# Streaming a table in transfers of two blocks instead of one, inside a decoder step on one core

## The chip, the cores and the metric

The kernel runs on one core of a Trainium2 chip. Its metric is the device time of one execution in microseconds (us). Three executions of the kernel before took 3694.8, 3695.88 and 3690.24 us, a median of 3694.8 us. A further execution was recorded by the hardware profiler; all rows shown here are of that one.

## The reference

One layer of a decoder is computed for 1024 prompt tokens and 64 sample tokens (8 sequences of 8) of width 1024. Two token mixers (a retention and a gated linear recurrence) are merged, projected and added to the input. Then comes the part that matters here, a retrieval from two tables of 16384 rows of 1024 float32 numbers, `peer_u` and `peer_v`. Each token selects 128 rows by the scores of its 8 heads, and the layer adds a weighted sum of the selected rows of `peer_v`:

```
s1, s2 = scores of the two halves of each head's query with 128 keys each
expert = 128 * e1 + e2          # the 16 best pairs of each of 8 heads: 128 rows per token
act = gelu(einsum('td,tkd->tk', x, u_tab[expert]))
out = einsum('tk,tkd->td', g * act, v_tab[expert])
x = x + g2 * out                # and a final normalisation by the row's mean square
```

## The kernel before

The kernel is a program written by hand for each engine, with semaphores between them: TensorE (PE), VectorE (DVE), ScalarE (ACT), GpSimd (POOL) and SyncE (SP), which issues most transfers. The mixers and the projections take the first part. The retrieval is spread over the whole second half.

**First table, rows by index.** POOL issues one indirect DMA for each token slot of a tile of 128 tokens (`gather`, L1472 to L1486): 128 rows of 4 KB, 512 KB in all, into one of 6 buffers `rows`. DVE multiplies each with the token's vector and sums (`dot`, L1689). There are 1088 of these for `peer_u`. For the sample tokens and the last two tiles of prompt tokens the second table is used in the same way: 320 more gathers, from `peer_v`, whose rows DVE adds up with their weights (`vrow`, L1699). The order of these jobs between DVE's other work is fixed by the table `stages()`.

**Second table, streamed.** For the other 768 prompt tokens, in 3 groups of 256 (`NDG` = 3, `GT` = 256), the whole table `peer_v` is read once in each group, as 128 blocks of 128 rows, and multiplied on PE with a matrix `W` that holds, for each row of the table, the weight that each of the 256 tokens gives it. One block is `vbuf[:, s, :]`, 128 partitions by 1024 numbers, 4 KB per partition. There are `VB` = 4 such buffers, used in turn. PE's `block_steps` (L2266) waits for the block's transfer on the semaphore `v_in[s]` (L2268), multiplies it in 8 pieces (L2273, `vacc<-W,vbuf`; the profile counts two matmuls for each), and then raises `v_used`. Over the 3 groups that makes 384 blocks, 96 turns of a loop over 4.

`W` is made as the stream runs. For each step of 4 tokens DVE and ACT build one-hot matrices (L1763, L1768, L2023, L2026), PE multiplies them in 12 small matmuls (`batch`, L2260, `scat`), and ACT copies the result into `W` (L2030). PE's order is: one block, one such batch, one block, and so on, in the first 320 blocks. The last 64 blocks (the second half of the last group) have no batch between them.

**SP's stream.** `v_stream` (L1373) holds the loop that issues the transfers. For buffer `s` it waits until the block that stood there has been used (L1376), and issues the next 512 KB (L1377). `v_used` starts at 4, so the first four are issued at once. Between parts of the stream SP issues other transfers on the same queue: a tile of `htok` (L1371), and in the last two groups the output of the group before (`y_store`, L1385, 1 MB) and the load of the next residual (`x3_load`, L1381, 1 MB), each 5 and 2 loop turns before a group's end; in the last group also two loads for the sample tokens (L1440, L1441) after 20 turns.

**The end.** After its last block PE multiplies the sample tokens' sums (L2390), for which DVE waits (L1832) before it goes on with its rows of `peer_v`; some 200 gathered rows are still to be added then, and two tiles to be finished.

Of the kernel before, what the change touches and what calls it, by code (L numbers as in the profile page):

```python
# [27 lines left out]
P = 128  # L28
D = 1024
# [16 lines left out]
NKEY = 128  # L46
# [24 lines left out]
VB, SB, VD = 4, 4, 6  # L71
QB = P // SB
# [157 lines left out]
def program(nc, I, O, S):  # L230
# [3 lines left out]
    def sem(name):  # L234
        return ctx.enter_context(nc.semaphore(name))

    def sb(c, name, shape, dt=F32):
        return c.enter_context(nc.sbuf_tensor(name, shape, dt))
# [17 lines left out]
    def hold(eng):  # L256

        eng.sem_inc(hold_sem, 1)

    with ctx:  # L260
# [43 lines left out]
        vbuf = sb(ctx, "vbuf", [P, VB, D])  # L304
# [964 lines left out]
        scaled2, q_ps, qh_ready, s_ps, s_ready, tr_ready, tr_free = (sem(n) for n in ("scaled2", "q_ps", "qh_ready", "s_ps", "s_ready", "tr_ready", "tr_free"))  # L1269
        tk, dk, pos_ready, hot_ready, idx_ready, max_ready, exp_ready = (sem(n) for n in ("tk", "dk", "pos_ready", "hot_ready", "idx_ready", "max_ready", "exp_ready"))  # L1270
        landed = [sem(f"landed{i}") for i in range(VD)]
        h_in, v_in = [sem("h_in0"), sem("h_in1")], [sem(f"v_in{i}") for i in range(VB)]
        used, v_used, gelu_ready, tr4_ready, picks_ready, oh_ready, sc_ps, w_evac, vacc_ready, ev_ready = (sem("s4_" + n) for n in (
            "used", "v_used", "gelu_ready", "tr4_ready", "picks_ready", "oh_ready", "sc_ps", "w_evac", "vacc_ready", "ev_ready"))
        x2g_in, sq4_ready, sums_ready, rs_ready, y_ready, y_out, ef_ready, acc_ready, oh2_ready, abs_ready, eq_ready = (sem("s4_" + n) for n in (
# [10 lines left out]
        def batch0(i):  # L1286
            return (i - FIRST_Q) * QB
# [64 lines left out]
        with nc.Block() as block:  # L1352
            @block.sync
            def _(sp):
# [17 lines left out]

                def v_stream(g, lo, hi):  # L1373
                    with sp.Fori(lo, hi) as i:
                        for s in range(VB):
                            sp.wait_ge(v_used, g * NKEY + i * VB + (s + 1))  # L1376
                            sp.dma_start(vbuf[:, s, :], I["peer_v"][bass.ds((i * VB + s) * P, P), :]).then_inc(v_in[s], 16)  # L1377

                def x3_load(g):
                    c0 = XG[g][0]  # L1380
# [52 lines left out]
                for g in range(NDG):  # L1433
                    h_load(2 * g + 3)
                    v_stream(g, 0, cut)
                    if g < NDG - 1:
                        h_load(2 * g + 4)
                    else:
                        sp.wait_ge(idx_ready, NUNIT)
                        sp.dma_start(spare, S["sums"]).then_inc(sum_out, 16)  # L1440
                        sp.dma_start(xs, S["x2"][:, :, FIRST:TA].rearrange("k p t -> p k t")).then_inc(xs_in, 16)  # L1441
                    if g:
                        v_stream(g, cut, end - 5)
                        y_store(g - 1)
                        v_stream(g, end - 5, end - 2)
                        sp.wait_ge(y_out, g * 16)
                        x3_load(g)
                        v_stream(g, end - 2, end)
                    else:
                        v_stream(g, cut, end)  # L1450
# [726 lines left out]
            def _(pe):  # L2177
# [75 lines left out]
                def batch(b, q, banks=scat):  # L2253
                    h = q % 2
                    pe.wait_ge(oh_ready, b + 1)
                    pe.wait_ge(oh2_ready, b + 2)
                    pe.wait_ge(w_evac, b + 1)
                    for n in range(SB):
                        for j in range(3):
                            mm = pe.matmul(banks[h][:, n * HK:(n + 1) * HK], oh2[:, h, n, :], oh1w[:, h, j, n // 2, :, n % 2], start=(j == 0), stop=(j == 2), skip_group_check=True)  # L2260
                    mm.then_inc(sc_ps, 1)

                def quarter(i4, scattering, inside=None):
                    g, q4 = divmod(i4, 4)

                    def block_steps(i, clear):  # L2266
                        for s in range(VB):
                            pe.wait_ge(v_in[s], g * (16 * NKEY // VB) + i * 16 + (q4 * (16 * QB // VB) + 16))  # L2268
                            e1 = slice(s, s + 1) if clear else bass.ds(i * VB + (q4 * QB + s), 1)
                            for k in range(KC):  # L2270
                                if clear and s == 0 and g and k % 2 == 0:
                                    pe.wait_ge(ev_ready, 4 * g + k // 2 - 3)
                                mm = pe.matmul(vacc[:, k, :], vbuf[:, s, k * P:(k + 1) * P], W[:, e1, :].rearrange("p o t -> p (o t)"),  # L2273
                                               start=(clear and s == 0 and k % 2 == 0), stop=False, skip_group_check=True)
                            mm.then_inc(v_used, 1)
                            if scattering:
                                batch(batch0(i4) + i * VB + s, s)
                    lo = 0
                    if q4 == 0:
                        block_steps(0, True)  # L2280
                        lo = 1
                    if inside is not None:
                        hold(pe)
                        with pe.Fori(lo, TURN_AT // VB) as i:
                            block_steps(i, False)
                        lo = TURN_AT // VB
                        inside()
                    hold(pe)
                    with pe.Fori(lo, QB // VB) as i:
                        block_steps(i, False)  # L2290
# [165 lines left out]
```

## Time and profile before

| | |
|---|---|
| median of 3 executions | 3694.8 us (3690.24 to 3695.88) |
| profiled execution, its own time | 3689.39 us |
| its span, first to last instruction | 3687.6 us |
| PE, DVE, POOL, ACT busy | 85%, 79%, 53%, 36% of the span |
| moved by DMA | 1127.21 MB, 305 GB/s read from and written to HBM over the span |
| of it the stream of `peer_v` | 384 transfers of 512 KB |
| mean granted clock of TensorE | 0.93 of full speed |

How to read it: the stream begins at 1752.6 us, PE's first block at 1770 us, and its last block ends at 3374 us. What bounds the kernel differs between the stretches inside this time, so each is read alone. Idle time of an engine matters only where what it waits for, or who waits for it, sets the end.

### The profile page before, as it was taken

Reading aid. Unit: us, or ns where it says so; the run is one execution under the profiler, and the core shown is the slowest. Engines: PE = TensorE matmul, PEld = TensorE weight load, DVE = VectorE, ACT = ScalarE, POOL = GpSimd, SP = SyncE. Lnnn points to the kernel's source line nnn. Section 1 sums busy time; section 2 is a strip of 40 time slices with the busy share of each in tenths; the row PEclk is TensorE's granted clock in tenths of the full one; section 3 lists DMA queues with packets and bytes.
Section 4 is the critical chain, followed back from the end, with each engine's and each line's share of the span. In section 5 each row is a group of like instructions: output and inputs, shape, how many; then the busy total and the mean of one; then the engine's idle time right before and its main releaser. Section 6 shows DMA issues by size and latency. Waiting matters only on the chain.

```text
span 3687.6 us, 56423 instructions
## 1 busy us (share of the span) xinstructions
PE 3124.7 (85%) x17498; PEld 2479.9 (67%) x17498; DVE 2906.8 (79%) x6210; ACT 1341.4 (36%) x2988; POOL 1954.9 (53%) x1504
## 2 busy tenths in 40 slices
PE   7999999999999989588899999999988999995000
PEld 4777776666666658477778788778877888884000
DVE  3333347998888877888899999999999887667898
ACT  4333311222222221178555555555555565000000
POOL 0000013454466654454677776767766766676676
PEclk9999999999999999799999999999999999997555
DMA  7444454777788898777999999999999999999998
GB/s 258 140 135 130 137 161 140 243 230 239 237 293 291 293 322 299 278 265 265 356 396 385 387 372 398 367 363 389 384 346 379 371 408 405 402 411 350 344 352 305
DMA packets 435382, 1127.21 MB, mean 306 GB/s; under 512 B 41888, under 2 KB 174368, under 8 KB 435232
## 3 DMA queue, kind: packets, MB, share of 16 engines
q0 software_dynamic: 204800, 745.10, 54.7%
q1 hardware_dynamic: 225664, 370.51, 28.2%
q10 hardware_dynamic: 4768, 9.96, 0.7%
q8 instruction: 49, 0.80, 0.1%
q14 instruction: 101, 0.83, 0.1%
HBM read 1098.81 MB, written 26.62 MB: 305 GB/s over the span
## 4 chain that ended last, share of the span: by engine, by line
PE 36%; DVE 24%; issue 13%; DMA 9%; POOL 3%; ACT 1%; DVEq 0%; ACTq 0%; POOLq 0%; SPq 0%
PE vacc L2273 16%; DVE rows L1689 10%; PE vacc L863 8%; DMA rows<-in_peer_u,eidx 5%; PE scat L2207 3%; DVE oh1w L1768 2%; PE vacc L834 2%; POOL rows L1486 2%; PE vacc L2187 2%; DMA rows<-in_peer_v,eidx 1%; DMA vbuf<-in_peer_v 1%; DVE eidf L1581 1%; PE scat L2260 1%; DVE htok L1699 1%; DVE hot L1675 1%
## 5 line engine op out<-in xcount | busy, mean ns | idle before, releaser
L1486 POOL DMA_INDIRECT rows<-in_peer_u,eidx x1088 | 1424.7, 1309 | 959.8 <-DVE dots L1689 602.6
L2273 PE MATMUL vacc<-W,vbuf 128*128 (+1 forms) x6144 | 1422.6, 387 | 34.3 <-DMA vbuf<-in_peer_v 23.2
L1689 DVE CUSTOM_DVE_ANT_0 rows<-rows,htok 128x1024 f32<-128x1024 f32 x1088 | 1349.9, 1269 | 126.3 <-DMA rows<-in_peer_u,eidx 115.4
L2273 PEld LDWEIGHTS vacc<-W,vbuf 128*128 128x128 f32 x6144 | 1154.9, 192 | 184.3 <-issue 36.1
L2023 ACT ACTIVATE oh<-iota,e2s 128x128 bf16<-128x128 f32 x1536 | 486.4, 391 | 17.0 <-DVE wpart L1739 9.8
L863 PE MATMUL vacc<-W 128*128 128x384 f32 x1280 | 435.1, 496 | 1.2 <-ACTq L763 1.2
L1470 POOL TENSOR_TENSOR hot<-hot,cid 128x864 f32<-128x864 f32 x68 | 129.2, 1903 | 543.3 <-DVE hot L1675 542.0
L1699 DVE SCALAR_TENSOR_TENSOR htok<-rows,dots,htok 128x1024 f32<-128x1024 f32 x256 | 328.8, 1284 | 72.9 <-DMA rows<-in_peer_v,eidx 66.3
L1486 POOL DMA_INDIRECT rows<-in_peer_v,eidx x256 | 310.4, 1212 | 121.4 <-issue 88.1
L863 PEld LDWEIGHTS vacc<-W 128*128 128x128 f32 x1280 | 242.8, 193 | 168.3 <-issue 9.5
L2030 ACT ACTIVATE W<-scat 128x256 f32 (+1 forms) x320 | 122.6, 383 | 580.7 <-PE scat L2260 534.1
L2026 ACT ACTIVATE oh<-oh,ones 128x512 bf16<-128x512 bf16 x384 | 277.2, 722 | 12.5
L1768 DVE TENSOR_TENSOR oh1w<-oh,wpart 128x768 bf16<-128x768 bf16 x384 | 237.7, 619 | 45.4 <-PE scat L2260 25.7
L2207 PE MATMUL scat<-W 128*128 128x256 f32 (+1 forms) x1024 | 252.5, 403 | 5.4 <-DVE W L1566 5.4
L2260 PEld LDWEIGHTS scat<-oh1w,oh 128*128 128x128 bf16 x3840 | 154.5, 97 | 118.3 <-issue 72.1
L2207 PEld LDWEIGHTS scat<-W 128*128 128x128 f32 x1024 | 196.9, 196 | 44.9 <-issue 6.3
L2260 PE MATMUL scat<-oh1w,oh 128*128 128x64 bf16 x3840 | 167.5, 192 | 58.6 <-DVE oh1w L1768 49.0
L863 PE MATMUL vacc<-rows,W 128*128 128x320 f32 x640 | 179.8, 436 | 2.5 <-ACTq L763 2.5
L2299 PE MATMUL vacc<-ident,htok 128*128 128x128 f32 x16 | 3.9, 424 | 209.8 <-DVEq L1802 209.8
L834 PE MATMUL vacc<-W 128*128 128x256 f32 x768 | 169.4, 381 | 0.0
L252 ACT ACTIVATE W<-vacc 128x768 f32<-128x768 f32 x32 | 25.9, 811 | 379.4 <-PE vacc L863 365.1
L834 PEld LDWEIGHTS vacc<-W 128*128 128x128 f32 x768 | 146.7, 191 | 23.2 <-ACTq L801 1.6
(330 smaller groups left out, 3086.9 us busy)
## 6 DMA issues: line engine op xcount, KB each, us to landing
vbuf<-in_peer_v SPq DMA_DIRECT2D x384, 512.0 KB
W<-in_w_in SPq DMA_DIRECT2D x80, 512.0 KB, 7.5
W<-in_wq SPq DMA_DIRECT2D x64, 512.0 KB
vbuf<-in_w_ada SPq DMA_DIRECT2D x9, 2048.0 KB, 24.1
rows<-in_peer_u,eidx POOLq DMA_INDIRECT x1088
W<-in_w_in SPq DMA_DIRECT2D x16, 1024.0 KB, 6.7
W<-in_w_ada SPq DMA_DIRECT2D x3, 2048.0 KB, 19.2
W<-in_w_out SPq DMA_DIRECT2D x12, 512.0 KB
```

Of the source, the lines that this page charges most:

```text
L834: mm = pe.matmul(dst, z.hnT[:, k, t * P:(t + 1) * P], w_qkv[:, k, :], start=(k == 0), stop=(k == KC - 1))
L863: mm = pe.matmul(pslice(z, pj if bank == "pj" else pk, s), w_part[j - 1][:, k, :], z.hnT[:, k, lo:hi], start=(k == 0), stop=(k == KC - 1))
L1470: g.tensor_tensor(hot[:, t, :, :], hot[:, t, :, :], bc(cid[:, t, :], 1, [P, TOPK, NCAND]), ALU.mult).then_inc(hot_ready, 1)
L1486: g.indirect_dma_start(rows[:, s, :], None, table[:, :], bass.IndirectOffsetOnAxis(ap=picked, axis=0)).then_inc(landed[s], 16)
L1689: v.tensor_tensor_reduce(rows[:, s, :], rows[:, s, :], htok[:, home, :], 1.0, 0.0, ALU.mult, ALU.add, dots_of(t)[:, c:c + 1]).then_inc(use ...
L1699: v.scalar_tensor_tensor(acc[t], rows[:, s, :], w[:, c:c + 1], acc[t], ALU.mult, ALU.add).then_inc(used, 1)
L1768: v.tensor_tensor(oh1w[:, h, :, :, :, :], bc(oh1[:, j % EB, :, :, :], 1, shp), bc(wpart[:, u * QB + j, :, :, :], 3, shp), ALU.mult).then_i ...
L2023: ins = act.activation(oh2[:, h, n, :], iota[:, :], ACT.Abs, bias=e2s[:, bass.ds(k, 1)], scale=-1.0)
L2026: act.activation(oh2[:, h, :, :], oh2[:, h, :, :], ACT.Relu, bias=ones[:, 0:1], scale=-1.0).then_inc(oh2_ready, 1)
L2207: mm = pe.matmul(scat[u][:, 0:n], wq[j % 4][:, k, :], hn2T[g][:, k, 0:n], start=(k == 0), stop=(k == KC - 1))
L2260: mm = pe.matmul(banks[h][:, n * HK:(n + 1) * HK], oh2[:, h, n, :], oh1w[:, h, j, n // 2, :, n % 2], start=(j == 0), stop=(j == 2), skip_g ...
L2273: mm = pe.matmul(vacc[:, k, :], vbuf[:, s, k * P:(k + 1) * P], W[:, e1, :].rearrange("p o t -> p (o t)"), start=(clear and s == 0 and k % ...
```

## The change

The host lays out a second copy of the table's contents, `v_pairs`, in place of reading `peer_v` for the stream. In it the rows of two successive blocks that go to the same partition lie behind each other, so that one partition's part of a pair is 8 KB in one piece. SP issues one transfer of 1 MB for a pair of buffers where it issued two of 512 KB. A pair is issued when both of its buffers have been used. There are 2 semaphores `v_in` in place of 4, one for each pair, and PE waits on the one of the block's pair. The number of buffers, the order of the blocks and everything on the other engines stay.

```diff
-        h_in, v_in = [sem("h_in0"), sem("h_in1")], [sem(f"v_in{i}") for i in range(VB)]
+        h_in, v_in = [sem("h_in0"), sem("h_in1")], [sem(f"v_in{i}") for i in range(VB // 2)]
 ...
                 def v_stream(g, lo, hi):
                     with sp.Fori(lo, hi) as i:
-                        for s in range(VB):
-                            sp.wait_ge(v_used, g * NKEY + i * VB + (s + 1))
-                            sp.dma_start(vbuf[:, s, :], I["peer_v"][bass.ds((i * VB + s) * P, P), :]).then_inc(v_in[s], 16)
+                        for h in range(VB // 2):
+                            sp.wait_ge(v_used, g * NKEY + i * VB + (2 * h + 2))
+                            src = I["v_pairs"][bass.ds(i * (VB // 2) + h, 1)].rearrange("o p n -> p (o n)")
+                            sp.dma_start(vbuf[:, 2 * h:2 * h + 2, :].rearrange("p s n -> p (s n)"), src).then_inc(v_in[h], 16)
 ...
                         for s in range(VB):
-                            pe.wait_ge(v_in[s], g * (16 * NKEY // VB) + i * 16 + (q4 * (16 * QB // VB) + 16))
+                            pe.wait_ge(v_in[s // 2], g * (16 * NKEY // VB) + i * 16 + (q4 * (16 * QB // VB) + 16))
 ...
         "peer_u": a["peer_u"][0], "peer_v": a["peer_v"][0],
+        "v_pairs": a["peer_v"][0].reshape(NKEY // 2, 2, P, D).transpose(0, 2, 1, 3).reshape(NKEY // 2, P, 2 * D),
```

SP's instructions for one part of the stream (a load of `htok`, then the loop of one turn) stood before as follows; `ISA` is the wait with the address, `DMA` the issue.

```order
156 L1371 DMA htok<-scratch_hn 128x1024
157 L1374 UNCONDITIONAL_BRANCH
158 L1374 ISA
159 L1377 ISA
160 L1377 DMA vbuf<-in_peer_v 128x1024
161 L1376 REGISTER_ALU
162 L1377 ISA
163 L1377 DMA vbuf<-in_peer_v 128x1024
164 L1376 REGISTER_ALU
165 L1377 ISA
166 L1377 DMA vbuf<-in_peer_v 128x1024
167 L1376 REGISTER_ALU
```

The same place of the changed kernel, on SP:

```order
150 L1371 DMA htok<-scratch_hn 128x1024
151 L1374 UNCONDITIONAL_BRANCH
152 L1374 ISA
153 L1378 ISA
154 L1378 DMA vbuf<-in_v_pairs 128x2048
155 L1376 REGISTER_ALU
156 L1378 ISA
157 L1378 DMA vbuf<-in_v_pairs 128x2048
158 L1374 REGISTER_ALU
159 L1374 COMPARE_AND_BRANCH
```

Two issues stand in one turn of the loop where there were four; what stands ahead of and behind the loop is the same. On PE (the two first blocks of a turn, inside the loop) the instructions of before are these:

```order
711 L2273 ISA [waits v_in0]
712 L2273 MATMUL vacc<-W,vbuf 128x256 x8
717 L2273 ISA [waits v_in1]
718 L2273 MATMUL vacc<-W,vbuf 128x256 x8
```

and now:

```order
711 L2274 ISA [waits v_in0]
712 L2274 MATMUL vacc<-W,vbuf 128x256 x8
717 L2274 ISA [waits v_in0]
718 L2274 MATMUL vacc<-W,vbuf 128x256 x8
```

The matmuls stay in place; the second block of a pair waits on the same semaphore as the first.

## Rows read from the trace of the kernel before

**Rows 1.** Page, slices: busy tenths of the DMA engines in 40 slices of 92 us.

```profile
DMA  7444454777788898777999999999999999999998
```

**Rows 2.** Busy time by stretch: start:end, length, engines (instructions), clock, DMA share, GB/s.

```profile
1760.00:2869.00 1109.00, 1031.24 (x7255) 883.02 (x7255) 1049.38 (x2496) 604.37 (x1579) 769.72 (x571) 0.99 0.98 377
2869.00:3125.00 256.00, 255.03 (x1808) 221.07 (x1807) 203.12 (x353) 147.87 (x381) 173.24 (x134) 0.99 1.00 395
3125.00:3375.00 250.00, 229.29 (x1034) 199.96 (x1033) 158.32 (x195) 2.21 (x4) 173.91 (x123) 0.96 1.02 403
3375.00:3688.00 313.00, 20.68 (x89) 17.41 (x88) 272.60 (x252) 8.07 (x12) 213.69 (x189) 0.52 0.90 328
```

**Rows 3.** Waits of PE alone from 2869 to 3374 us: total us, times, longest.

```profile
PE vacc L2273 <- DMA vbuf<-in_peer_v: 20.7, 3, 7.9
...
```

**Rows 4.** Chain that ended last, around PE's late blocks: start, length, what.

```profile
3170.17 15.38 DMA vbuf<-in_peer_v
...
3275.21 17.50 DMA vbuf<-in_peer_v
...
3326.45 17.90 DMA vbuf<-in_peer_v
...
3374.24 1.75 PE tps L2390 x16
```

**Rows 5.** The same chain by line, from 1760 to 2868 us (first lines' start).

```profile
by line: DVE rows L1689 21.2%; issue 19.7%; DMA rows<-in_peer_u,eidx 17.8%; PE vacc L2273 14.2%; DVE oh1w L1768 6.3%; POOL rows L1486 2.6%; DVE hot L1675 2.3%; DVE oh L1763 2.2%; DVE eidf L1581 2.0%; PE scat L2260 1.7%; DVE ti L1634 0.9%; D
```

**Rows 6.** DVE in order of time, the row after PE's last block.

```profile
3376.01 0.69 DVE L1832 TENSOR_TENSOR hot<-tps,g2T 128x512 f32<-128x512 f32 x1 [8.51 <-PE tps L2390]
```

**Rows 7.** Issues of L1377 from 3005 to 3110 us, then 3190 to 3270 us.

```profile
L1377 SPq DMA_DIRECT2D vbuf<-in_peer_v x27: 332/333/333, 3006.3 to 3107.5; - x27
...
L1377 SPq DMA_DIRECT2D vbuf<-in_peer_v x23: 332/333/333, 3192.3 to 3268.3; - x23
```

**Rows 8.** PE's three waits for the stream, one window each (3165, 3270, 3325 us).

```profile
PE vacc L2273 <- DMA vbuf<-in_peer_v: 5.4, 1, 5.4
...
PE vacc L2273 <- DMA vbuf<-in_peer_v: 7.5, 1, 7.5
...
PE vacc L2273 <- DMA vbuf<-in_peer_v: 7.9, 1, 7.9
```

**Rows 9.** DMA issues: count, KB each, median us from issue to landing.

```profile
W<-in_w_in SPq DMA_DIRECT2D x16, 1024.0 KB, 6.7
W<-in_dmask SPq DMA_DIRECT2D x1, 512.0 KB, 4.8
```

**Rows 10.** DMA queues: packets, MB, share of 16 engines; 60 to 300, 2940 to 3125 us.

```profile
q1 hardware_dynamic: 42442, 30.99, 43.5%
...
q0 software_dynamic: 13889, 50.58, 68.9%
q1 hardware_dynamic: 6765, 24.64, 33.5%
```

**Rows 11.** Page, all packets of the run by size.

```profile
DMA packets 435382, 1127.21 MB, mean 306 GB/s; under 512 B 41888, under 2 KB 174368, under 8 KB 435232
q8 instruction: 49, 0.80, 0.1%
q14 instruction: 101, 0.83, 0.1%
```

**Rows 12.** SP in order of time around an output store in the stream.

```profile
3272.30 0.40 SPq L1385 DMA_DIRECT2D out_y<-x  x1
3275.21 48.13 SPq L1377 DMA_DIRECT2D vbuf<-in_peer_v  x12
```

**Rows 13.** Waits from 1760 to 2869 us, of DVE and of PE.

```profile
DVE rows L1689 <- DMA rows<-in_peer_u,eidx: 43.1, 64, 5.7
...
PE scat L2260 <- DVE oh1w L1768: 48.5, 43, 6.5
PE vacc L2273 <- DMA vbuf<-in_peer_v: 2.5, 1, 2.5
```

## The prediction

> **What bounds the kernel now.** I read the slices first: from slice 20 on the DMA engines are 9 tenths or more busy [rows 1], so the stream of the table and the gathers share a full resource. By stretch [rows 2], the reader is to see three regimes. From 1760 to 2869 us DVE is busy 1049 of 1109 us and PE 1031. From 2869 to 3125 us PE is busy 255.0 of 256 us. From 3125 to 3375 us PE is busy 229 of 250 us, and DMA's share is 1.02. After that it is the tail of gathers.
>
> Then PE's waits: from 2869 us to its last block it waits for hardly anything but the stream, 20.7 us in 3 places [rows 3]. Then the chain: in the last stretch it runs through PE's blocks and these three transfers, up to L2390 at 3374.24 us [rows 4]. There DVE has stood idle for 8.51 us until PE delivers [rows 6], and what follows it is gathers and DVE work that the change does not touch. So from 2869 to 3374 us every microsecond that PE loses moves the end. Before 2869 us the chain is mixed, DVE's rows 21.2%, gathers' landings 17.8%, PE's blocks 14.2% [rows 5], and PE has slack.
>
> **PE's pace.** 27 issues of the stream from 3006.3 to 3107.5 us are 26 intervals of 3.89 us: one block with its batch. 23 issues from 3192.3 to 3268.3 us are 22 intervals of 3.455 us: one block alone [rows 7].
>
> **What the change takes from the stream: its lead.** A block's transfer is issued when the block four earlier is used, so it has three blocks' time until PE needs it. The three waits show the lead without batches exactly: transfers landing 15.38, 17.50 and 17.90 us after issue [rows 4] made PE wait 5.4, 7.5 and 7.9 us [rows 8], so the lead is 10.0 us, 0.35 under 3 x 3.455. Now a pair goes out when both its blocks are used, and its first block is needed two blocks later: 10.0 - 3.455 = 6.55 us without batches. With batches it is 2 x 3.89 = 7.8 us (the batch covers the 0.35).
>
> **What it adds: a longer transfer.** How long 512 KB of the stream take is in no row; in 13 of the last 16 turns of the loop PE did not wait, so under 10.0 us. I build it up. A packet's time: 42442 packets of 30.99 MB take 43.5% of 16 x 240 us, 39.4 ns at 730 bytes; 13889 packets of 50.58 MB take 68.9% of 16 x 185 us, 146.8 ns at 3642 bytes [rows 10]. The line through both is 12.4 ns + 0.0369 ns per byte: 164 ns for 4 KB, 315 ns for 8 KB. One engine of 16 moves 8 rows of a block. A transfer of 1 MB with no gathers beside it landed after 6.7 us [rows 9]; its data alone need 16 x 0.164 = 2.6 us, which leaves 4.1 us fixed. (The one of 512 KB after 4.8 us leaves 3.5.) Beside full gathers I let the two queues take packets in turn: a block needs 8 x (0.164 + 0.164) = 2.6 us, 6.7 in all; a pair in packets of 8 KB needs 8 x (0.315 + 0.164) = 3.8, 7.9 in all; a pair in packets of 4 KB 5.2, 9.3 in all. That nothing above 4 KB goes out on this kernel's data queues is seen in the page: just 150 packets have 8 KB or more, as many as the instruction queues have [rows 11]. So no row shows an 8 KB packet of data. I take 7.9, since the row is contiguous on both sides, and keep 6.7 and 9.3 as ends.
>
> The turn by packets is also what the Trainium skill states ("DMA: Bandwidth & Descriptors", section Queues, rings and completion order): each engine goes round its queues packet by packet. The rows agree in so far as both queues together make 102.4% of the engines' time [rows 10]; they don't show the order. The same page (Anatomy of one DMA) fits 2.0 us plus bytes at 436 GB/s, so a pair would land after 4.4 us and never be late. The trace's 1 MB took 6.7 us without contention [rows 9], so I go by the trace.
>
> **The sum.**
> (a) Last 64 blocks, 16 turns, 13 of them without a foreign transfer. A turn is two pairs. The first waits 7.9 - 6.55 = 1.35 us; the second has gained those 1.35 us of lead and waits for nothing; then the first is late again. 13 x 1.35 = +17.6 us. Ends: 13 x 0.15 = 2 and 13 x 2.75 = 36.
> (b) The 3 turns behind foreign transfers. SP issues the store at 3272.30 us and the block 2.9 us after it [rows 12]. The pair goes out 3.455 us later than that block did, but what it stands behind in the queue is the store, and PE needs its first block at the same moment; it lands later by its own extra 1.2 us only. 3 x 1.2 = +3.7. Ends 0 and 3 x 2.6 = 8.
> (c) 16 turns from 2869 to 3125 us: 7.9 - 7.8 = 0.1 each, +1.6. Ends 0 and 16 x 1.5 = 24.
> (d) Before 2869 us, 64 turns. At 0.1 us they are nothing beside PE's own idle time of 78 us [rows 2]. Two foreign transfers there cost PE 2.5 us before [rows 13], and get 1.2 us longer each; DVE, in front by up to a batch, takes most of it: +1. Behind PE's waiting block stand its next batch and so DVE's L1768, which waits for it; that is the price if the cover is gone. Upper end by 9.3 us: 64 x 1.5 = 96 us on PE, of which the chain's share of PE, 14.2 + 1.7% [rows 5], makes 15.
> (e) DMA time saved: 192 x 8 packets fewer on each engine, 1536 x 12.4 ns = 19 us over 1604 us, 13 of them before 2869 us. It helps where a landing binds, 17.8% of the chain [rows 5]: -2.3, rounded -3 with the halved number of issues. Lower end -13, since DVE waits 43.1 us for rows there [rows 13]. After 2869 us it helps nobody, since PE is the bound.
> SP's halved issues, at 0.33 us each [rows 7], cost nothing before or now: SP waits for PE between them.
>
> Sum: 17.6 + 3.7 + 1.6 + 1 - 3 = +21. On the profiled execution's 3689.4 us that is 3710; it lay 5.4 us under the median, and a median stands against a median, so the time is 3694.8 + 21 = **3716 us**.
>
> **Rivals.**
> *Packets of 4 KB.* If the 8 KB row is cut in two, a pair lands after 9.3 us: 36 + 8 + 24 + 15 + 1 - 3 = +81, 3776 us. For it: no data packet above 4 KB in the run [rows 11]. Against it: none was asked for. The Trainium skill ("DMA: Bandwidth & Descriptors", section SWDGE vs HWDGE vs iDMA) has a packet at preferably 4096 bytes at most, told of the software path; no run here shows it for SP's queue.
> *Gathers pushed aside.* An 8 KB packet of the stream holds a waiting gather packet up by 0.151 us more, 8 times, 1.2 us per pair. If DVE can't make it good in the second half of the pair, 138 pairs before 2869 us at the 17.8% of the chain that landings hold add 29 us: 3745. Against it: DMA's total is no larger, and six buffers smooth it.
> *No change.* If the fixed part under load is the 3.5 us of the smaller transfer [rows 9], a pair lands after 7.3: (a) is 13 x 0.75 = 10, (c) is 0, (b) and (d) 5, and (e) takes -10: +5, 3700.
> *Faster.* DMA is the true bound, at 0.98 to 1.02 in all three stretches [rows 2], and PE's busy time only follows it. Then the 19 us saved count nearly in full, once a pair lands under 6.55 us: +4 from (b), -17, that is -13: 3682 us. The point from which it decides is 6.55 us. Against it: PE's 255 of 256 us busy, and 6.7 us for 1 MB alone. The skill's rule to batch to 1 MiB and more (same page, Rules for kernel authors) speaks for it; this stream has no idle queue that larger transfers could fill.
>
> **Chances.** Forecast 0.55 (its own range 3704 to 3732), 4 KB packets 0.17, gathers pushed aside 0.09, no change 0.11, faster 0.08. The range that holds 8 in 10 reaches over the no-change case below and to the 4 KB case above: 3695 to 3780. A difference of 0.2%, 7.4 us, is about what can be told from none. Faster by more: 0.09; within: 0.15; slower by more: 0.76.
>
> **What would show it.** In the last stretch PE waits for `vbuf` about 16 times and not 3, near 1.35 us each, every second pair, and the three long ones grow by about 1.2. PE's last block ends near 3395 us, DVE's idle time at L1832 grows from 8.5 to about 30, and what comes after keeps its length. From 2869 to 3125 us PE stays near 3.89 us per block. Queue 1 shows packets of 8 KB with 315 ns; if they are of 4 KB, the 4 KB rival holds. If PE waits for nothing new and DVE's waits for rows fall, the forecast is wrong and DMA was the bound; if DVE's waits for rows rise before 2869 us, the gathers were pushed aside.

## The result, and the profile after

The changed kernel takes 3747.55 us (4 runs, 3746.25 to 3748.23) against 3694.81 before: a ratio of 1.0145, interval 1.013 to 1.0159, or 53 us more. The forecast was 3716 us, slower by 21, with a range of 3695 to 3780. The direction and the range held. The size did not: it was two and a half times the forecast. The profiled execution has a span of 3746.2 us, 58.6 more than the one of before.

The page of the changed kernel first: packets of all queues by size, the two data queues, and the stream's issues. The last two lines are the data queues of the kernel before.

```profile
DMA packets 407733, 1127.19 MB, mean 301 GB/s; under 512 B 38816, under 2 KB 171296, under 8 KB 383008
q0 software_dynamic: 204800, 745.10, 54.3%
q1 hardware_dynamic: 198016, 370.50, 27.5%
vbuf<-in_v_pairs SPq DMA_DIRECT2D x192, 1024.0 KB
...
q0 software_dynamic: 204800, 745.10, 54.7%
q1 hardware_dynamic: 225664, 370.51, 28.2%
```

Now 24725 packets have 8 KB or more, where there were 150 [rows 11]: 24576, which is 192 x 128, more than the instruction queues' 149. Each partition's 8 KB goes out as one packet, as forecast. Queue 1 (the stream's) fell from 28.2% of 3687.6 us to 27.5% of 3746.2 us, 10 us less for each of the 16 engines. Queue 0 (the gathers') went from 54.7% to 54.3%, which is 17 us more. (The shares are rounded, so each difference is good to about 4 us.) So the saving in packets is real, and it did not shorten the queues' work as a whole.

Busy time by stretch of the changed kernel, with the columns of [rows 2]. The stretches are PE's blocks 0 to 255 (two groups), 256 to 319 (third group, with batches), 320 to 383 (without), and the tail:

```profile
1772.00:2889.00 1117.00, 1034.92 (x7196) 884.93 (x7196) 1037.29 (x2464) 593.35 (x1550) 752.31 (x567) 0.98 0.96 371
2889.00:3159.00 270.00, 257.64 (x1807) 222.03 (x1808) 202.81 (x356) 151.84 (x392) 152.37 (x133) 0.99 0.98 379
3159.00:3433.00 274.00, 237.12 (x1029) 199.56 (x1028) 158.34 (x195) 2.52 (x4) 138.66 (x123) 0.95 0.93 369
3433.00:3746.00 313.00, 22.00 (x97) 18.36 (x95) 272.67 (x252) 8.07 (x12) 214.44 (x189) 0.53 0.91 328
```

The tail has kept its 313 us. The third group's second half took 274 us against about 250, its first half 270 against 256, and the two groups ahead of them 1117 against about 1098 (from 1770 to 2868 us before). PE is no longer busy all the time in the third group's first half, and DMA's share fell in every stretch ahead of the tail, by 0.02, 0.02 and 0.09.

PE's waits for the stream in the last stretch (total, times, longest), the three long ones and two turns of the loop, PE in order of time:

```profile
PE vacc L2274 <- DMA vbuf<-in_v_pairs: 36.6, 20, 8.4
...
3225.64 2.92 PE L2274 MATMUL vacc<-W,vbuf 128*128 x6 [5.33 <-DMA vbuf<-in_v_pairs]
...
3345.85 3.78 PE L2274 MATMUL vacc<-W,vbuf 128*128 x8 [7.67 <-DMA vbuf<-in_v_pairs]
...
3402.09 8.27 PE L2274 MATMUL vacc<-W,vbuf 128*128 x23 [8.40 <-DMA vbuf<-in_v_pairs]
```

```profile
3261.13 7.17 PE L2274 MATMUL vacc<-W,vbuf 128*128 x32 [0.93 <-DMA vbuf<-in_v_pairs]
3268.51 7.17 PE L2274 MATMUL vacc<-W,vbuf 128*128 x32 [0.21 <-issue]
3276.76 7.17 PE L2274 MATMUL vacc<-W,vbuf 128*128 x32 [1.08 <-DMA vbuf<-in_v_pairs]
3284.30 7.17 PE L2274 MATMUL vacc<-W,vbuf 128*128 x32 [0.37 <-DMA vbuf<-in_v_pairs]
```

The three long waits stayed what they were [rows 8], 5.4, 7.5 and 7.9 us then. The new waiting is in the other 17, 15.2 us. Each row of x32 is a pair: PE halts before each, about 1 us before one of a turn and 0.2 to 0.4 us before the other, and a turn takes 3276.76 - 3261.13 = 15.6 us where four blocks took 13.8.

The chain of the changed kernel in these stretches, start, length and what (a landing stands here only when PE waited for it):

```profile
3049.59 9.25 DMA vbuf<-in_v_pairs
3066.87 8.31 DMA vbuf<-in_v_pairs
...
3275.86 8.31 DMA vbuf<-in_v_pairs
3284.30 7.18 PE vacc L2274 x32
3291.65 8.01 DMA vbuf<-in_v_pairs
3299.80 7.18 PE vacc L2274 x32
3307.14 7.79 DMA vbuf<-in_v_pairs
```

The landings that PE waited for took 7.8 to 9.3 us in these rows, and 7.7 to 9.4 us in all of the third group, leaving out those behind a foreign transfer. How long the others took is in no row. And the place where DVE meets PE's last block, which answers to [rows 6]; ahead of it stand DVE's waits up to 2869 us (those of [rows 13] are 43.1 us, 64 times):

```profile
DVE rows L1690 <- DMA rows<-in_peer_u,eidx: 65.5, 60, 4.8
...
3434.79 0.69 DVE L1833 TENSOR_TENSOR hot<-tps,g2T 128x512 f32<-128x512 f32 x1 [43.88 <-PE tps L2391]
```

The last row and the one of before divide the loss. L1833 starts 58.8 us later than it did. 35.4 of them are DVE's longer idle time (43.9 against 8.5). The other 23.4 are DVE's own arrival: it came to this point at 3390.9 us and not at 3367.5, and its waits for gathered rows had grown by 22.4 us. So two paths became late, PE's more than DVE's. If PE's waits alone were taken away, DVE's 23.4 less the old slack of 8.5 should still move the end by 15 us; a run below tests this. The forecast had nothing there.

### The profile page after: what moved, and what is told of

Same layout as the page of the kernel before. It is cut to its first block, busy times and chain, and to the rows that moved or that the text cites. A ratio compares the mean times of both kernels' runs of the same rounds, so it can differ in the third digit from the quotient of the medians.

```text
span 3746.2 us, 55655 instructions
## 1 busy us (share of the span) xinstructions
PE 3147.2 (84%) x17498; PEld 2488.7 (66%) x17498; DVE 2905.0 (78%) x6210; ACT 1340.8 (36%) x2988; POOL 1898.4 (51%) x1504
## 3 DMA queue, kind: packets, MB, share of 16 engines
q0 software_dynamic: 204800, 745.10, 54.3%
q1 hardware_dynamic: 198016, 370.50, 27.5%
## 4 chain that ended last, share of the span: by engine, by line
PE 28%; DVE 21%; issue 17%; DMA 16%; POOL 3%; ACT 1%; SPq 0%; ACTq 0%; DVEq 0%; POOLq 0%
PE vacc L2274 10%; DMA rows<-in_peer_u,eidx 8%; DVE rows L1690 7%; PE vacc L863 7%; DMA vbuf<-in_v_pairs 5%; POOL rows L1487 3%; PE scat L2208 3%; PE vacc L834 2%; DVE oh1w L1769 2%; PE vacc L2188 2%; DMA rows<-in_peer_v,eidx 2%; DVE eidf L1582 1%; DVE htok L1700 1%; DVE oh L1764 1%; DVE hot L1676 1%
## 5 line engine op out<-in xcount | busy, mean ns | idle before, releaser
L1487 POOL DMA_INDIRECT rows<-in_peer_u,eidx x1088 | 1386.5, 1274 | 1026.2 <-DVE dots L1690 674.3
L2274 PE MATMUL vacc<-W,vbuf 128*128 (+1 forms) x6144 | 1440.0, 389 | 79.5 <-DMA vbuf<-in_v_pairs 65.4
L1487 POOL DMA_INDIRECT rows<-in_peer_v,eidx x256 | 292.4, 1142 | 170.0 <-issue 123.8
```

Of the source, the lines that this page charges most:

```text
L1487: g.indirect_dma_start(rows[:, s, :], None, table[:, :], bass.IndirectOffsetOnAxis(ap=picked, axis=0)).then_inc(landed[s], 16)
```

## The experiments

Theory A: a pair is issued too late and lands too late for PE. Rival B: the stream in pairs makes the gathers land late, and DVE with them. Each ratio is to the kernel before on the same chip.

**One half of the change, the late issue.**

```diff
-                            sp.wait_ge(v_used, g * NKEY + i * VB + (s + 1))
+                            sp.wait_ge(v_used, g * NKEY + i * VB + (2 * (s // 2) + 2))
```

> The kernel before with one edit: two transfers of 512 KB as before, but both are issued only when both buffers of the pair have been used. So the lead of a pair's first block falls by one block as in the change, the packets stay at 4 KB and PE still waits for each block alone. Theory A (the lead is too short for the landing, once per turn of the loop): the first block lands after about 6.7 us, against a lead of 6.4 us without batches and 7.6 with: 13 x 0.3 = 4 us in the last 64 blocks, little before, in all +3 to +10 us, 3698 to 3705. Rival B (packets of 8 KB hold up the gathers, the lead does not matter): 0, 3695. Rival C (the late issue by itself, whatever the size, is the loss): near the changed kernel, 3740 to 3750.

Measured: 3711.55 us, ratio 1.0053 (1.0035 to 1.0071), some 19 us. The late issue alone, at 4 KB and 512 KB, makes a good third of the change's loss. It is more than A's +3 to +10, B's zero is out, and so is C, the whole loss. PE's waits for the stream from 2880 us on:

```profile
PE vacc L2273 <- DMA vbuf<-in_peer_v: 29.4, 11, 9.8
```

**The other dose of lateness.** Each block one block later, nothing bunched:

```diff
-                            sp.wait_ge(v_used, g * NKEY + i * VB + (s + 1))
+                            sp.wait_ge(v_used, g * NKEY + i * VB + (s + 2))
```

> The kernel before with one edit: each block's transfer of 512 KB is issued one block later, so its lead is two blocks in place of three; nothing is bunched, packets stay at 4 KB. Theory A (lead against landing): a block lands after 6.7 us against 6.4 without batches, so PE waits 0.3 us once in three blocks of the last 64, 6 us, and the landings that lie above the median add as much again: +5 to +20 us, 3698 to 3713. If issuing two transfers at once was what cost the run with late issue its 19 us: 0 to +5.

Measured: 3712.88 us, 1.0057 (1.004 to 1.0074). The same loss with nothing bunched. PE waited 33.4 us in 13 places from 2880 us on, and DVE's waits for gathered rows stayed at 46.3 us up to 2900 us (before: 47.4). So a lead of two blocks does not suffice where PE sets the pace, even with a transfer of 512 KB. But it is only just too short for the stream's own blocks: 3.9 us in ten places here, and 2.9 us in eight in the run before this one. The three waits behind foreign transfers make the rest, 29.5 and 26.5 us where they were 20.7. (Here a foreign transfer is issued one block later as well.) DVE's arrival at L1832 was 3375.0 us with the late issue and 3367.7 here, against 3367.5 before. That does not yet show a cost of bunching, since DVE's arrival differs by up to 8 us between traces whose first two groups have the same stream.

**The packet size.** The changed kernel, reading the pair straight from the table:

```diff
-                            src = I["v_pairs"][bass.ds(i * (VB // 2) + h, 1)].rearrange("o p n -> p (o n)")
+                            src = I["peer_v"][bass.ds((i * VB + 2 * h) * P, 2 * P), :].rearrange("(s p) n -> p s n", p=P)
```

(the destination is `vbuf[:, 2 * h:2 * h + 2, :]` with its two rows apart).

> The changed kernel with one edit: a pair is read straight from the table as it was, two pieces of 4 KB per partition in one transfer of 1 MB, so packets should be of 4 KB. Lead as in the change. Theory A: a pair lands after 9.3 us and not 7.9, so PE waits 9.3 + 0.15 - 6.55 = 2.9 us in each of 13 turns of the last 64 blocks (38), about 1.7 in each of the 16 turns before (27), and some 0.9 of it shows in the 64 turns ahead (60): +125 us, 3820, range 3780 to 3850. Rival B (8 KB packets hold up the gathers): the gathers get half of each engine again, so it is faster than the changed kernel, 3700 to 3740.

Measured: 3770.97 us, 1.0221 (1.0197 to 1.0246), +78 us. The direction is A's: smaller packets, later landing, slower. The size is two thirds of what A said and lies below its range. That one wait per turn at full size counts too much once both pairs are late, since every wait lengthens the next lead, is my reading and not tested. By the ratios the layout by pairs is worth some 28 us against the same transfer without it (1.0221 against 1.0145), yet the pair costs more.

**Where it is lost.** Pairs in some groups only:

```diff
+        PAIRED = (0, 1)     # and (2,) in the second kernel
...
+                        if g in PAIRED:
+                            for h in range(VB // 2):
+                                sp.wait_ge(v_used, g * NKEY + i * VB + (2 * h + 2))
+                                src = I["v_pairs"][bass.ds(i * (VB // 2) + h, 1)].rearrange("o p n -> p (o n)")
+                                sp.dma_start(vbuf[:, 2 * h:2 * h + 2, :].rearrange("p s n -> p (s n)"), src).then_inc(v_in[2 * h], 16)
+                        for s in range(VB if g not in PAIRED else 0):
```

> Pairs in the first two groups of the stream only (256 blocks), single blocks in the third. Theory A in the size that the changed trace shows: PE is 21 us late at block 256 there, and nothing is added after it: +21 us, 3716 (3708 to 3722). If DVE sets the pace there and has slack for PE's waits: 0 to +5. If lateness made there is what makes the third group slow: +45 to +53.

> Pairs in the third group only (128 blocks), single blocks in the first two. Theory A: 13 us over the 64 blocks with batches and about 22 over the 64 without, +35 us, 3730 (3722 to 3738); with the run of pairs in groups 1 and 2 it adds up to the change's +53. My prediction's own terms (a), (b), (c) would give +23, 3718. Rival B: the gathers' delay counts where DVE is the bound, in the first two groups, so here only 0 to +10.

Measured: first two groups 3709.1 us, 1.0047 (1.0029 to 1.0065), +17; third group 3725.32 us, 1.0089 (1.0069 to 1.0108), +33. They add up to 50 of the change's 53, and each came out near what A said; for the first two groups that was for another reason, as the runs with constant tiles show. The third group's part is in PE's waits (42.0 us, 34 times, from 2880 us on) and in DVE's idle time for L2391's counterpart (39.5 us). In the first two groups PE waited too, 33.5 us in 34 places up to 2900 us, but what DVE waited for was rows (this profiled execution took 3717.04 us, 8 more than the median):

```profile
DVE rows L1695 <- DMA rows<-in_peer_u,eidx: 71.9, 64, 4.8
DVE oh1w L1774 <- PE scat L2266: 3.7, 4, 1.2
```

**PE's lead taken out of the question.** The long matmuls read a constant tile, so that the sum over the second table is left out; every transfer is made as before, and PE asks for the landing only ahead of the last matmul:

```diff
-                            pe.wait_ge(v_in[s // 2], ...)
...
+                                if k == KC - 1 and s % 2:
+                                    pe.wait_ge(v_in[s // 2], ...)
-                                mm = pe.matmul(vacc[:, k, :], vbuf[:, s, k * P:(k + 1) * P], ...
+                                mm = pe.matmul(vacc[:, k, :], ident[:, :], ...
```

> The changed kernel, with PE's long matmuls reading a constant tile in place of the streamed blocks (so the sum over the second table is left out), the transfers unchanged and issued as before; PE asks for a pair's landing only ahead of the last matmul of the pair's second block, 6.9 to 7.8 us later than it did. All DMA traffic, packets of 8 KB and late issue stay; only PE's short lead is taken away. To be compared with the same edit of the kernel before, which runs beside it. Theory A (PE's lead): the two are equal within 5 us, both near 3680 to 3690, since part of the three long waits goes too. Rival B (8 KB packets or bunched transfers hold up the gathers): this one stays 20 to 50 us above the other.

> The kernel before with the same edit (PE reads a constant tile, the sum over the second table is left out), the landing of each block asked for ahead of the block's last matmul. Three long waits of 5.4, 7.5 and 7.9 us become about 2, 4 and 4.5: 10 us less than before, 3685. Same under both theories; it is the level for the other run.

Measured: pairs 3703.24 us, 1.0025 (1.0013 to 1.0038); single blocks 3688.48 us, 0.9988 (0.9977 to 0.9998). So 15 us of the 53 stay when PE hardly waits for the stream (in the pairs' run 7.5 us in 3 places from 2880 us on), and 38 go. Both theories hold a part. The 15 us are the size worked out above from DVE's arrival, and the trace of the pairs' run agrees: DVE comes to L1833 at 3388.98 us without waiting for PE, where it came at 3390.9 in the changed kernel.

```profile
3388.98 0.68 DVE L1833 TENSOR_TENSOR hot<-tps,g2T 128x512 f32<-128x512 f32 x1
```

(The profiled execution of the single blocks was the slowest of its ten, 3701.55 us, so its trace is not set beside this one.) The same form for three more ways to move the table:

> The transfer of 1 MB in packets of 4 KB (pair read straight from the table), with PE's long matmuls reading a constant tile (the sum over the second table is left out) and PE asking for the landing only at a pair's end. It tells what the 15 us are that the changed kernel keeps in this form. Theory B8 (an 8 KB packet holds gather packets up): with 4 KB packets it falls to the level of single blocks in this form, 3688. Theory BB (1 MB at once, in whatever packets, bunches the gathers): it stays at 3703.

> Two transfers of 512 KB issued together when both buffers of a pair are used, in packets of 4 KB, PE's long matmuls reading a constant tile (the sum over the second table is left out), landing asked for ahead of each block's last matmul. Theory B8: 3688, since no packet is above 4 KB. Theory BB: 3700 to 3705, since the same 1 MB is queued at once; it should then equal the run with one transfer of 1 MB in 4 KB packets.

> Pairs in the first two groups only, PE's long matmuls reading a constant tile (the sum over the second table is left out), landing asked for ahead of the last matmul of a pair's first block. If the first two groups' 17 us come from gathers that land later while DVE sets the pace: 12 to 17 us over the single blocks in this form (3688), 3700 to 3706. If they come from PE's waits for the stream: 3688, +-4.

Measured: one transfer of 1 MB in 4 KB packets 3697.11 us, 1.0018 (1.0009 to 1.0028); two of 512 KB issued together 3694.73 us, 1.0015 (1.0003 to 1.0027); 8 KB pairs in the first two groups only 3705.12 us, 1.0045 (1.0028 to 1.0062). The last is as slow as the same pairs with PE reading them (1.0047), though PE waited for the stream 5.5 us up to 2900 us there and not 33.5. So the loss of the first two groups is not PE's waiting; it sits there and on the gathers' side. The two forms in 4 KB packets lie clear above single blocks (0.9988), by 11 and 10 us, and the intervals do not part them from the 8 KB form (1.0025, 14 us by the ratios). So most of what stays in this form needs no packet of 8 KB. One thing stays open: pairs in two groups only came out above pairs in all three. PE asks for the landing one block earlier there, and the intervals overlap.

**The first two groups alone, three forms on one chip.** The 8 KB kernel is the one above again; the others have the pair from the table in one transfer, and two transfers issued together:

```diff
-                            sp.wait_ge(v_used, g * NKEY + i * VB + (s + 1))
+                            sp.wait_ge(v_used, g * NKEY + i * VB + ((s + 1) if g == 2 else (2 * (s // 2) + 2)))
```

> Pairs in the first two groups only, each one transfer of 1 MB read straight from the table, in packets of 4 KB; single blocks in the third group. If 8 KB packets hold the gathers up: 0 to +6 us, though a pair lands about 1.3 us later and PE waits more often than with 8 KB. If 1 MB queued at once does it: +12 to +20. If PE's waits do it after all: above the run with 8 KB packets.

> Pairs of the changed kernel, in packets of 8 KB, in the first two groups only; the same kernel as in the earlier run of pairs in groups 1 and 2, here beside the two others on one chip. +17 us (+12 to +22).

> Two transfers of 512 KB issued together once a pair's two buffers are used, in the first two groups only; packets of 4 KB. If 8 KB packets are the cause: 0 to +4 us. If 1 MB queued at once is: +12 to +20, like the run with one transfer in 4 KB packets.

Measured: 1 MB in 4 KB packets 3725.73 us, 1.0095 (1.0082 to 1.0108); in 8 KB packets 3711.2 us, 1.0053 (1.0039 to 1.0066); two of 512 KB 3699.6 us, 1.0021 (1.0012 to 1.0029), which is +8 and lies between the two sizes expected. The first surprised me: in 4 KB packets the same transfer is worse here too. The chains of the 4 KB and the 8 KB form up to 2868 us, shares by line, say why:

```profile
by line: PE vacc L2281 45.5%; DMA vbuf<-in_peer_v 35.1%; issue 7.6%; PE scat L2266 3.2%; DVE rows L1695 2.1%; another core or an unknown queue 1.0%; DVE oh1w L1774 0.7%; SPq L1380 0.6%; DVE oh L1769 0.4%; DVE x L1802 0.3%; ACT L2020 0.2%; A
```

```profile
by line: DMA rows<-in_peer_u,eidx 30.3%; issue 28.7%; DVE rows L1695 12.3%; POOL rows L1492 6.5%; DVE oh1w L1774 3.4%; PE vacc L2281 2.7%; DVE eidf L1587 2.6%; DVE oh L1769 2.3%; DMA vbuf<-in_v_pairs 2.3%; DVE hot L1681 1.7%; DVE tv L1638 0
```

With 4 KB packets the bound passes to PE and the stream (81% of the chain), and PE waited for it 76.7 us in 52 places up to 2900 us. Before, DVE and its gathers held the larger part of a mixed chain [rows 5]. With 8 KB packets the stream is 2.3% of it and the gathers' landings are 30.3%, against 17.8 [rows 5]. DVE's waits for rows tell the same, of the 4 KB form first, then the 8 KB form, then two transfers together, up to 2900 us (before: 47.4 us, 69 times):

```profile
DVE rows L1695 <- DMA rows<-in_peer_u,eidx: 39.8, 44, 5.4
```

```profile
DVE rows L1695 <- DMA rows<-in_peer_u,eidx: 67.4, 59, 4.6
```

```profile
DVE rows L1689 <- DMA rows<-in_peer_u,eidx: 56.3, 65, 4.7
```

(In three other runs whose stream is that of before in these groups they were 50.5 to 53.9 us.) So 8 of the 20 us on this chip come with the late, bunched issue alone. The other 12 come with one transfer of 8 KB packets. They run through the gathers by the chain. That it is the packet's length that holds them up is not shown: the control with 4 KB packets is bound by something else here, and where PE reads a constant tile the packet size made no difference clear of noise.

**The three long waits, another place.** The foreign transfers (L1385, L1381, L1440, L1441) are issued from ACT:

```diff
-                        v_stream(g, cut, end - 5)
-                        y_store(g - 1)
-                        v_stream(g, end - 5, end - 2)
-                        sp.wait_ge(y_out, g * 16)
-                        x3_load(g)
-                        v_stream(g, end - 2, end)
+                        v_stream(g, cut, end)
```

> The kernel before, with the transfers that stand between the stream's on SP's queue (two loads for the sample tokens, the output stores of 1 MB and the loads of the next residual) issued from ACT, on its own queue. The stream is then not behind them in a queue. If the three waits of 5.4, 7.5 and 7.9 us come from standing behind in one queue: they go, 20.7 us of PE's chain, and with them 1 to 2 us each of low clock after them: 3665 to 3676. If they come from sharing the engines: nothing, 3695. ACT's queue as a third one in turn may also slow gathers: up to 3705.

> The changed kernel with the same move to ACT's queue. Theory A: the long waits go, the short one in every turn of the loop stays, so it gains about as much as the kernel before does by this edit, 20 to 27 us: 3722 to 3730, and stays some 50 us above the other run. If the loss of the change lay in the turns behind the foreign transfers, it would fall to the other run's time.

Measured: on the kernel before 3689.9 us, 0.9991 (0.9981 to 1.0001); on the changed kernel 3716.76 us, 1.0061 (1.0044 to 1.0078). In the first, PE waits for the stream nowhere from 2880 us on: the 20.7 us were waits behind foreign transfers in one queue. (ACT issues them at other moments too, the store at 3142.1 and not at 3272.3 us, but still among the stream's blocks.) But the time hardly moved, 3 us. PE is done 23 us earlier and DVE no longer waits for it; DVE and its gathers were only 8.5 us behind as the bound, and in this trace they came to the place at 3375.2 us, 7.7 later than before. I had expected 20 to 30 and had not looked at who comes next. In the changed kernel the same edit brings 31 us, since there DVE waited 44 us for PE. So on top of this edit the pairs cost 27 us, where 50 was expected. The short waits stay, and no long one:

```profile
PE vacc L2283 <- DMA vbuf<-in_v_pairs: 26.1, 32, 2.1
```

The first of these is no slower than the kernel before, but it isn't shown to be faster, so no version here beats it clearly.

## Why the prediction was right or wrong

The mechanism forecast for the third group, a lead that is too short once per turn, was right. What failed is the first two groups, forecast at -2 us and measured at 17 to 20, and the term for the third group's first half, forecast at 1.6 and measured at 14.

**The bound** was read rightly for the third group: PE from 2869 us on, with DVE waiting at L1832. Pairs there alone cost 33 us; PE waited 21 us longer for the stream, and DVE 31 us longer for PE.

**The lead** was right: the pair issued at 3371.69 us was needed at 3378.42, 6.7 us later, against 6.55. The landing of 7.9 us, in one packet of 8 KB for each row, was right as a typical value of those that PE waited for, but partly by luck. Its fixed part of 4.1 us was taken from a load of 1 MB as if that went in rows of 4 KB. L376 moves it in rows of 1 KB, 64 for each engine; by the prediction's own line these need 3.2 us, which leaves 3.5 fixed and puts a pair at 7.3, the case of no change. (The fit from which the prediction has 4.4 us, in the Trainium skill, "DMA: Bandwidth & Descriptors", section Anatomy of one DMA, is stated for transfers that GpSimd issues, and the stream is SP's; no landing of a pair in these rows was under 7.7.) The 4 KB case would have been the later landing that was forecast (8.3 to 10.3 us in its trace, against 9.3), and is slower as forecast (+78 against +81), though by a path through both bounds.

**Term (a)**, 17.6 us in 13 turns: the waits measure 15.2 us, in 17 places. The second pair of a turn, forecast to wait for nothing, waits a little too. But the stretch grew by 24 us. The rest is in no wait: a pair that PE begins after a halt takes 7.17 us where two blocks took 6.91, and the mean clock of the stretch was 0.95 where it had been 0.96. Why the matmuls take longer is not shown.

**Term (b)**, +3.7 us: measured 5.33, 7.67, 8.40 against 5.4, 7.5, 7.9, +0.6.

**Term (c)**, +1.6 us for 16 turns, was mis-sized: 270 against 256 us, +14. What PE waited for from 2889 to 3159 us:

```profile
PE vacc L2274 <- DMA vbuf<-in_v_pairs: 4.1, 5, 1.5
PE vacc L2274 <- issue: 3.6, 6, 1.2
PE scat L2261 <- DVE oh1w L1769: 2.8, 1, 2.8
```

The 6 waits without a named releaser stand before the first block of a pair as well, so up to 7.7 us are late landings. Some 4 us more went on waits for DVE and ACT, and 2.6 us on matmuls that took longer (257.6 us busy against 255.0). The step that failed is taking one number, 7.9, from another, 7.8. The landings that PE waited for in this stretch took 8.2 to 9.3 us. One that comes in time brings nothing back, and a late one costs its whole excess. A margin near zero has a price of its own, and it covers about half of the 14 us.

**Terms (d) and (e)**, together -2 us, failed in kind. Measured 17 and 20 us in the two runs with pairs in these groups. I priced PE's waits and saved packet time there, and put the gathers' later landing at nothing. PE's waits were indeed covered: with them removed the loss stays. The saved packet time brought nothing: queue 1 took 10 us less for each engine and not 19, and queue 0 took 17 more. What happened has the mark of a rival that I had given a chance of 0.09, gathers pushed aside: DVE's waits for rows rose from 43.1 to 65.5 us. (Its price of 29 us counts 138 pairs; the first two groups have 128, which makes it 27.) But its mechanism, a gather packet held up by a longer packet of the stream, is not shown: 8 of the 20 us come with 4 KB packets, when two transfers are issued together, and for the other 12 the cause stays open. I had dismissed the rival since the total of bytes is no larger and six buffers smooth it; the rows of before already showed DVE waiting 64 times for a landing, and at those times there was no landed row in stock for a burst to draw on.

**The rivals on the other side** fell. No change: the time rose by 53 us. Faster, with DMA as the true bound: its share was near full, but it went down with the pairs, and the fewer packets gave no time back.

## What to carry to other kernels

Where buffers are few, the size of a transfer and its lead are one quantity: to join two buffers' transfers takes one block of lead (here from 10.0 to 6.7 us) and adds the second half's time to the landing. Compare the lead with the late landings and not with the median, and count a margin near zero as a loss. When a second path is 8 us behind the bound, a gain on the bound is worth 8 us at most (20.7 us of PE's waits removed brought 3), and a change in a shared queue has to be priced on both paths.

## What the runs showed of the hardware

A row of 8 KB contiguous on both sides went out from SP's queue as one packet (24576 of them). The same bytes in two pieces of 4 KB, as a transfer of the same size, went out as packets of 4 KB (no packet of 8 KB is left but the 149 of the instruction queues), and the kernel took some 28 us more (by the ratios). With pairs on one queue and gathers on the other, DMA's mean share fell from 0.98 to 0.96, from 1.00 to 0.98 and from 1.02 to 0.93 in the three stretches, though the stream moved its bytes in less packet time: with PE late, its transfers were issued late. Pairs in 8 KB packets in the first two groups raised DVE's waits for gathered rows to 61.7 us and more in each of the six runs that had them (up to 2900 us; from 47.4 to 53.9 with the stream of before). And a store of 1 MB in the same queue made a block behind it land after 17.5 us in place of under 10; from another engine's queue it cost the stream no wait at all, though it was issued at another moment. In the kernel before, TensorE had stood idle for 5.4, 7.5 and 7.9 us in its three long waits; in the 7 to 8 us around and after their ends its granted clock was 0.55, 0.68 and 0.73, so a part of each stretch ran at the lower level, 1.2 GHz. From 3125 to 3375 us it was 0.96.
